# The output bias written into PSUM ahead of the output projection, with residuals, loads and banks moved around it

## The chip, the cores and the metric

The kernel runs on the eight cores of one Trainium2 chip. Every core computes one of the eight batch elements, and no core talks to another. The metric is the device time in microseconds of the slowest core. A line such as L517 names a line of the kernel before.

## The reference

For each batch element x is 4096 x 1024 in float32. One layer is computed, then a last RMSNorm:

```python
h = rmsnorm(x, norm_g)
proj = h @ w_in + b_in                       # 1024 -> 2816 columns
q, k, v, z_a, u, v_s, z_s = split(proj)      # 512,128,128,512,512,512,512
attn = banded_sink_attention(q, k, v, sinks) * silu(z_a)     # window 128, blocks of 128
sgu  = gelu(u) * (W_s @ layernorm(gelu(v_s)) + b) * silu(z_s) # chunks of 128
x = x + concat(attn, sgu) @ w_out + b_out
return rmsnorm(x, final_norm_g)
```

## The kernel before, in words

The 4096 rows of a core are eight stages of 512, and each stage is four tiles (or attention blocks) of 128 rows. A stage has these steps. The rows are loaded into `xa`, squared on ACT (L468), scaled to bf16 `xn` (L482, L483) and transposed into `xT`. TensorE then forms projections from `xT` in groups of eight matmuls, 512 columns each, one PSUM bank per group (`fm_group`, L517): four groups for q, one for k, four for u, four for z_s and four for z_a; v (L542) and v_s (L571) are formed row by row. ACT or DVE takes a group out of PSUM and adds its bias (L523, L524, L527). Attention of a block needs scores (L647), exp on ACT (L652), a mask (L665 on DVE or L660 on POOL), the sum of the two masked halves (L682), the products with v and with ones (L674, L677), ln and exp on ACT (L690, L694), and two multiplications (L696, L701) that end in `mixT`. The gating branch (L617 to L629) fills the other half of `mixT`.

The output of a row tile (`out_tile`) is two halves of 512 columns. For each half eight matmuls (L725) write one bank, and DVE adds the bank to the residual in `xe` (L730). ACT squares the tile (L733), POOL makes the reciprocal root in two small steps (L735, L737), DVE scales (L739) and SP stores it (L742). The residual is a second load of the same rows of x into `xe` (`load_xe`, L709), after which POOL adds the output bias to the whole tile in place (L711). `xe` has four tile slots, one for each tile of a stage; a slot is loaded again only when its store has been read out.

The order of instructions on every engine is fixed when the program is built. `Scheduler.run` is a list scheduler: it walks through time with a cost for each operation, takes the operation that can start first, and settles ties by a priority number. It also deals out the eight PSUM banks, by classes with caps: `CAPS = {"S": 4, "V": 2, "P": 4}`, where S is a pair of banks for scores, V the two banks of one attention block, and P all other groups, the output halves among them. ACT runs in phases per stage (gelu, silu, exp), with a table load between them (L424); the matmuls of a gelu or silu group are held back by `gate` until their phase is the current one or about to be. Each engine then runs its list in order, and waits for semaphores where an operand comes from elsewhere.

Setup: SP loads the 22 weight blocks of w_in through four slots of `xe` and four of `mixT`, POOL's own queue loads `w_out` with a cast to bf16 (L777, eight loads), and SP loads the small constants, among them `gf_sb` and `bout_sb` (L420).

## Time and profile before

| what | value |
|---|---|
| median of 3 runs | 534.2 us (534.0 to 534.81) |
| the profiled execution, its own time | 536.34 us |
| span of its slowest core (core 0), first to last instruction | 534.8 us |
| spans of all cores | 528.0 to 534.8 us |
| PE / DVE / ACT / POOL busy, share of the span | 90% / 71% / 61% / 36% |
| DMA, mean over the span | 137 GB/s |

The profile is of one execution. The span leaves out 1.5 us of that execution's own time. An engine that is busy for a small share of the whole can still set the end in one stretch, so the windows and the timeline are read beside the averages. Releasers in brackets say which instruction ended an idle time.

### The profile page before, as it was taken

The numbers are of one execution on the slowest core, as the hardware profiler recorded it, in microseconds if no ns is written. First come the engines' busy times: TensorE is split into PE (matmuls) and PEld (weight loads), VectorE is DVE, ScalarE is ACT, GpSimd is POOL, SyncE is SP. The second block draws the span as 40 slices with busy tenths as digits, with TensorE's granted clock in tenths as the row PEclk, the third lists the DMA queues.
The fourth block names the chain that finished last, engine by engine and source line by source line (L and its number), as shares of the span: only waits on it lengthen the run. The fifth ranks groups of instructions, "written<-read, shape, count | busy, mean of one in ns | idle before, by whom it ended". The sixth has DMA issues, their size and how long they took to land.

```text
span 534.8 us, 9042 instructions; the slowest of 8 cores (528.0 to 534.8 us)
## 1 busy us (share of the span) xinstructions
PE 483.6 (90%) x2802; PEld 221.5 (41%) x2852; DVE 379.2 (71%) x527; ACT 325.6 (61%) x565; POOL 191.6 (36%) x232
## 2 busy tenths in 40 slices
PE   1799986898999999999999999999999999999960
PEld 0357442344444434444444434443444435443320
DVE  1676889659778767778775597766757687557963
ACT  4363393855677475847675756858578575348621
POOL 1030564125023331333236254542364215450444
PEclk9999997999999999999999999999999999999985
DMA  7999993593008801336532933356342213300363
GB/s 233 329 344 324 313 232 50 106 253 116 1 40 203 230 1 40 120 66 172 159 104 59 210 101 119 119 94 146 126 152 65 51 63 136 119 1 39 120 182 132
DMA packets 44543, 73.12 MB, mean 137 GB/s; under 512 B 27600, under 2 KB 27728, under 8 KB 44496
## 3 DMA queue, kind: packets, MB, share of 16 engines
q1 hardware_dynamic: 43200, 70.40, 44.5%
q0 software_dynamic: 1152, 2.10, 2.4%
q8 instruction: 23, 0.38, 0.3%
q14 instruction: 24, 0.20, 0.1%
q10 hardware_dynamic: 144, 0.05, 0.1%
HBM read 51.56 MB, written 16.78 MB: 128 GB/s over the span
## 4 chain that ended last, share of the span: by engine, by line
PE 79%; issue 5%; DVE 4%; ACT 4%; POOL 3%; DMA 3%; SPq 0%; POOLq 0%; DVEq 0%; ACTq 0%
PE pp L517 40%; PE pp L725 18%; PE pp L571 9%; PE pp L674 3%; PE pp L647 3%; PE pp L542 2%; DMA xa<-x 2%; PE pp L556 1%; DMA xe<-x 1%; PE pp L677 1%; PE pp L617 1%; DVE PT L665 1%; DVE xe L739 1%; POOL w_out_bf L777 1%; ACT PT L652 1%
## 5 line engine op out<-in xcount | busy, mean ns | idle before, releaser
L517 PE MATMUL pp<-xT,w_fm 128*128 128x512 bf16 x1056 | 243.0, 382 | 6.9 <-DVE sgt L625 1.6
L517 PEld LDWEIGHTS pp<-xT,w_fm 128*128 128x128 bf16 x1088 | 104.2, 98 | 134.8 <-issue 15.9
L725 PE MATMUL pp<-w_out_bf,mixT 128*128 128x512 bf16 x497 | 117.8, 384 | 6.2 <-DVE mixT L701 3.8
L711 POOL TENSOR_TENSOR xe<-xe,bout_sb 128x1024 f32<-128x1024 f32 x32 | 77.4, 2423 | 29.7 <-DMA xe<-x 29.6
L725 PEld LDWEIGHTS pp<-w_out_bf,mixT 128*128 128x128 bf16 x512 | 47.9, 99 | 69.1 <-issue 18.0
L733 ACT ACTIVATE junk<-xe 128x1024 bf16<-128x1024 f32 x32 | 34.0, 1062 | 53.8 <-DVE xe L730 48.5
L730 DVE TENSOR_TENSOR xe<-pp,xe 128x512 f32<-128x512 f32 x64 | 43.4, 685 | 28.9 <-PE pp L725 24.1
L652 ACT ACTIVATE PT<-pp 128x1024 bf16<-128x1024 f32 x63 | 62.6, 1030 | 0.9 <-PE pp L647 0.9
L571 PE MATMUL pp<-w_vs,xT 128*128 128x512 bf16 x221 | 53.7, 391 | 6.6 <-DVE v_r L546 5.3
L739 DVE SCALAR_TENSOR_TENSOR xe<-xe,st_fr,gf_sb 128x1024 f32<-128x1024 f32 x32 | 47.1, 1473 | 15.4 <-POOL st_fr L737 9.5
L665 DVE TENSOR_TENSOR PT<-PT,pack_b_sb 128x1024 bf16<-128x1024 bf16 x57 | 50.4, 898 | 4.8 <-ACT PT L652 4.0
L690 ACT ACTIVATE LR<-pp,esink 128x128 f32<-128x128 f32 x128 | 36.3, 365 | 26.7 <-PE pp L677 26.0
L578 ACT ACTIVATE vs_f<-vs_f 128x512 f32<-128x512 f32 x32 | 19.6, 627 | 42.0 <-DVE vs_f L576 40.5
L735 POOL TENSOR_SCALAR st_fm<-st_fs 128x1 f32<-128x1 f32 x32 | 9.9, 309 | 95.9 <-ACT junk L733 95.4
L527 ACT ACTIVATE zaT<-pp,pack_a_sb 128x512 bf16<-128x512 f32 x32 | 21.7, 691 | 33.5 <-PE pp L517 32.2
L576 DVE TENSOR_TENSOR vs_f<-pp,bvs_sb 128x512 f32<-128x512 f32 x32 | 22.0, 688 | 26.1 <-PE pp L571 21.9
L468 ACT ACTIVATE junk<-xa 128x1024 bf16<-128x1024 f32 x32 | 33.7, 1055 | 6.0 <-DMA xa<-x 5.2
L571 PEld LDWEIGHTS pp<-w_vs,xT 128*128 128x128 bf16 x224 | 21.8, 100 | 35.5 <-issue 11.9
L629 POOL TENSOR_TENSOR mixT<-sgt,uT 128x512 bf16<-128x512 f32 x19 | 22.0, 1156 | 40.6 <-DVE sgt L625 33.8
L625 DVE SCALAR_TENSOR_TENSOR sgt<-pp,pack_b_sb,Cmat 128x512 f32<-128x512 f32 x32 | 23.2, 745 | 16.5 <-PE pp L617 8.9
L584 POOL TENSOR_SCALAR st_ve<-st_mv 128x1 f32<-128x1 f32 x32 | 8.5, 266 | 71.0 <-DVE st_mv L582 70.1
L424 ACT ACT_TABLE_LOAD x24 | 30.8, 1283 | 1.9 <-POOL ones L439 1.5
(63 smaller groups left out, 542.6 us busy)
## 6 DMA issues: line engine op xcount, KB each, us to landing
...
w_out_bf<-w_out POOLq DMA_DIRECT2D x8, 256.0 KB, 15.7
...
```

What stands on the lines that cost most here:

```text
L424: return lambda e: e.activation(out=dmy[:, 1:2], in_=dmy[:, 0:1], func=func)
L468: G.op("act", lambda e: e.activation(out=junk[:], in_=xa[:, tt, :], func=AF.Square, accum_out=st_ss[:, par, tt:tt + 1]), reads=[("xa", tt) ...
L517: ins = e.matmul(bank(h), lhsT=w_fm[:, FM.index(cb), k, :], rhs=xT[:, xb, k, :], start=(k == 0), stop=(k == 7))
L571: ins = e.matmul(bank(h), lhsT=xT[:, xb, k, tt * 128:(tt + 1) * 128], rhs=w_vs[:, k, :], start=(k == 0), stop=(k == 7))
L652: G.op("act", lambda e, h=h, kb=kb: e.activation(out=PT[:, p2, kb, :], in_=bank2(h), func=AF.Exp, scale=0.125), uses=[h], writes=[("PT", p ...
L665: return e.tensor_tensor(out=v, in0=v, in1=mask[kb].unsqueeze(1).to_broadcast([128, 8, 128]), op=ALU.mult)
L690: ins = e.activation(out=LR[:, lb, c * 128:(c + 1) * 128], in_=bank(hd)[:, c * 128:(c + 1) * 128], func=AF.Ln, bias=esink[:, c:c + 1])
L711: G.op("pool", lambda e: e.tensor_tensor(out=xe[:, s, :], in0=xe[:, s, :], in1=bout[:], op=ALU.add), reads=["c_bout"], writes=[("xe", s, 0 ...
L725: ins = e.matmul(bank(h), lhsT=mixT[:, mb, ec, tt * 128:(tt + 1) * 128], rhs=w_out[:, ec, hf * 512:(hf + 1) * 512], start=(ec == 0), stop= ...
L730: G.op("dve", lambda e, hf=hf, h=h: e.tensor_tensor(out=xe[:, s, hf * 512:(hf + 1) * 512], in0=bank(h), in1=xe[:, s, hf * 512:(hf + 1) * 5 ...
L733: G.op("act", lambda e: e.activation(out=junk[:], in_=xe[:, s, :], func=AF.Square, accum_out=st_fs[:, s:s + 1]), reads=[("xe", s, 0), ("xe ...
L739: G.op("dve", lambda e: e.scalar_tensor_tensor(out=xe[:, s, :], in0=xe[:, s, :], scalar=st_fr[:, s:s + 1], in1=gf[:], op0=ALU.mult, op1=AL ...
```

## The change

Six edits go together.

1. *Bias in PSUM.* POOL's addition of the bias (L711, 32 of them) goes. In its place ACT or DVE, whichever the scheduler finds free, copies 512 columns of the bias into the bank of an output half, 64 copies in all, and the eight matmuls of the half accumulate onto it (`start=False`). The copy reads the same inputs as the half needs, so it comes only when these are there. These banks are a class of their own, E, with a cap of 2, and they are only taken where the bank's last use wrote all of it by matmuls (`full`, `onto`). Where one bank is filled in pieces, only the first piece has `start` set.
2. *Last residual in `xa`.* The last stage has no load after it, so its rows are still in `xa`; its four tiles add onto `xa`, and are stored from there. Four loads of 512 KB go.
3. *Last silu inputs in SBUF.* The eight z groups of the last stage lose their gate. ACT or DVE takes them out of PSUM with their bias, into unused room of `xT` and of the q weights, and ACT applies silu from SBUF.
4. *`w_out` ahead of residual loads.* `gf_sb`, the first four loads of `xe` and the loads of `xa` for stage 2 all wait for the last load of `w_out`.
5. *Three V banks* instead of two.
6. *Port order.* A POOL operation marked `port` also waits for the DVE operation marked `port` that the scheduler placed ahead of it; L739 is now marked so.

```diff
-    CAPS = {"S": 4, "V": 2, "P": 4}
+    CAPS = {"S": 4, "V": 3, "P": 4, "E": 2}
...
+                    if b.onto and not all(bank_full[c] for c in cells):
+                        continue
...
             if o.port and e in ("dve", "pool"):
-                port[0] = free[e]
+                if e == "pool" and port[1] is not None and port[1].eng == "dve" and port[1] not in o.deps:
+                    o.deps.append(port[1])
+                port[:] = [free[e], o]
...
-            G.op("pe", mm, reads=[("xT", xb, t) for t in range(4)] + [("w", cb)], cost=1.73, alloc=[h], prio=prio, mode="full", gate=ph)
+            pre = st == NS - 1 and func == AF.Silu
+            G.op("pe", mm, reads=[("xT", xb, t) for t in range(4)] + [("w", cb)], cost=1.73, alloc=[h], prio=prio, mode="full",
+                 gate=None if pre else ph)
...
+                G.op({"dve": (0.745, lambda e: e.tensor_scalar(out=mem, in0=bank(h), scalar1=bias, scalar2=None, op0=ALU.add)),
+                      "act": (0.69, lambda e: e.activation(out=mem, in_=bank(h), func=AF.Identity, bias=bias))},
+                     None, uses=[h], reads=["c_biasfm"], writes=[("pre", i)], prio=prio, behind=[r for k in old for r in G.rd[k]])
+                G.op("act", lambda e: e.activation(out=dst, in_=mem, func=func), reads=[("pre", i)], writes=[key], cost=0.6,
+                     prio=prio - 0.3, phase=ph)
...
-            G.op("pool", lambda e: e.tensor_tensor(out=xe[:, s, :], in0=xe[:, s, :], in1=bout[:], op=ALU.add),
-                 reads=["c_bout"], writes=[("xe", s, 0), ("xe", s, 1)], cost=2.6, prio=st + 0.6 + 0.1 * s, port=True)
...
+            buf, key = (xa, ("xa", s)) if last else (xe, ("xe", s))
             for hf in range(2):
-                h = Bank("P")
...
+                h = Bank("E", onto=True)
...
+                fb = lambda e, h=h, cols=cols: e.activation(out=bank(h), in_=bout[:, cols], func=AF.Copy)
+                fv = lambda e, h=h, cols=cols: e.tensor_copy(out=bank(h), in_=bout[:, cols])
+                G.op({"act": (0.61, fb), "dve": (0.6, fv)}, None, reads=need + ["c_bout"], alloc=[h], prio=v0 - 0.2)
...
+                                       start=False, stop=(ec == 7), skip_group_check=True)
...
-            load_const("c_gf", gf[:], gf_d, eng="sp", kb=512, prio=-0.3, after=[w_op[21]])
+            load_const("c_gf", gf[:], gf_d, eng="sp", kb=512, prio=-0.3, after=[w_op[21]], reads=[("w_out", 7)])
...
         for cb in range(NCB):
             load_w(cb)
+        load_w_out()
...
         for tt in range(4):
-            load_xe(4 * (NS - 1) + tt)
             out_tile(4 * (NS - 1) + tt)
```

How the order moves, at three places. In the changed program L654, L694, L711, L658, L573, L725 and L604 are the old L625, L665, L682, L629, L546, L696 and L576; L757 is the new copy of the bias on DVE, L766, L730 and L775 are the old L730, L701 and L739, and L738, L440 and L431 the loads of L709, L429 and L420.

DVE, first attention stage, before (the masks of stage 0 and the v of stage 1):

```order
L625 SCALAR_TENSOR_TENSOR sgt<-pp,pack_b_sb,Cmat 128x512 [waits s_dve,s_pool,s_pe]
L523 TENSOR_SCALAR kT<-pp,pack_a_sb 128x512 [waits s_pe]
L665 TENSOR_TENSOR PT<-PT,pack_b_sb 128x1024 [waits s_act] x4
L682 TENSOR_TENSOR PC<-PT 128x1024 [waits s_dve]
L629 TENSOR_TENSOR mixT<-sgt,uT 128x512
L546 TENSOR_TENSOR v_r<-pp,pack_b_sb 128x512 [waits s_pe]
L625 SCALAR_TENSOR_TENSOR sgt<-pp,pack_b_sb,Cmat 128x512 [waits s_dve]
L576 TENSOR_TENSOR vs_f<-pp,bvs_sb 128x512 [waits s_pe]
```

DVE, the same place, with the change:

```order
L654 SCALAR_TENSOR_TENSOR sgt<-pp,pack_b_sb,Cmat 128x512 [waits s_dve,s_pool,s_pe]
L549 TENSOR_SCALAR kT<-pp,pack_a_sb 128x512 [waits s_pe]
L654 SCALAR_TENSOR_TENSOR sgt<-pp,pack_b_sb,Cmat 128x512 [waits s_dve,s_pool]
L694 TENSOR_TENSOR PT<-PT,pack_b_sb 128x1024 [waits s_act] x3
L711 TENSOR_TENSOR PC<-PT 128x1024 [waits s_dve]
L658 TENSOR_TENSOR mixT<-sgt,uT 128x512
L573 TENSOR_TENSOR v_r<-pp,pack_b_sb 128x512 [waits s_pe]
L694 TENSOR_TENSOR PT<-PT,pack_b_sb 128x1024 [waits s_act]
```

Three masks instead of four stand ahead of v_r, as one went to POOL, and the fourth sgt has moved ahead of them.

SP, the loads after the weights, before (`xa` is for stage 2, `xe` for the residual of stage 0; two more of `xe` follow):

```order
L420 DMA bout_sb<-bout_bc 128x1024
L420 DMA gf_sb<-gf_bc 128x1024
L429 DMA xa<-x 128x1024 [waits d_xa0,s_act]
L429 DMA xa<-x 128x1024 [waits d_xa1,s_act]
L429 DMA xa<-x 128x1024 [waits d_xa2,s_act]
L429 DMA xa<-x 128x1024 [waits d_xa3,s_act]
L709 DMA xe<-x 128x1024 [waits d_xe0,s_dve]
L709 DMA xe<-x 128x1024 [waits d_xe1,s_dve]
```

SP, the same place, with the change:

```order
L431 DMA bout_sb<-bout_bc 128x1024
L431 DMA gf_sb<-gf_bc 128x1024 [waits d_wo7]
L738 DMA xe<-x 128x1024 [waits d_xe0,s_dve]
L738 DMA xe<-x 128x1024 [waits d_xe1,s_dve]
L738 DMA xe<-x 128x1024 [waits d_xe2,s_dve]
L440 DMA xa<-x 128x1024 [waits d_xa0,s_act]
L738 DMA xe<-x 128x1024 [waits d_xe3,s_dve]
L440 DMA xa<-x 128x1024 [waits d_xa1,s_act]
L440 DMA xa<-x 128x1024 [waits d_xa2,s_act]
```

The load of gf waits for the last piece of `w_out` (d_wo7), and everything after it on SP stands behind that wait; the residual loads have moved ahead of those of `xa`.

DVE, last stage, before, around the attention blocks 2 and 3:

```order
L739 SCALAR_TENSOR_TENSOR xe<-xe,st_fr,gf_sb 128x1024 [waits s_pool,s_act]
L739 SCALAR_TENSOR_TENSOR xe<-xe,st_fr,gf_sb 128x1024 [waits s_pool,s_act,s_dve]
L701 TENSOR_TENSOR mixT<-pp,LR 128x4x128 [waits s_pool,s_pe]
L739 SCALAR_TENSOR_TENSOR xe<-xe,st_fr,gf_sb 128x1024 [waits s_pool,s_dve,s_act]
L696 TENSOR_TENSOR LR<-LR,zaT 128x512 [waits s_act]
L730 TENSOR_TENSOR xe<-pp,xe 128x512 [waits s_pool,s_pe]
L701 TENSOR_TENSOR mixT<-pp,LR 128x4x128 [waits s_dve,s_pe]
L730 TENSOR_TENSOR xe<-pp,xe 128x512
L739 SCALAR_TENSOR_TENSOR xe<-xe,st_fr,gf_sb 128x1024 [waits s_pool,s_dve,s_act]
L730 TENSOR_TENSOR xe<-pp,xe 128x512 [waits s_pool,s_pe]
```

DVE, last stage, with the change, around the same blocks:

```order
L766 TENSOR_TENSOR xe<-pp,xe 128x512 [waits s_pe]
L694 TENSOR_TENSOR PT<-PT,pack_b_sb 128x1024 [waits s_act]
L725 TENSOR_TENSOR LR<-LR,zaT 128x512 [waits s_act]
L766 TENSOR_TENSOR xe<-pp,xe 128x512 [waits s_pe,d_xe3]
L730 TENSOR_TENSOR mixT<-pp,LR 128x4x128 [waits s_dve,s_pe]
L757 COPY pp<-bout_sb 128x512 [waits s_pe]
L711 TENSOR_TENSOR PC<-PT 128x1024 [waits s_pool]
L725 TENSOR_TENSOR LR<-LR,zaT 128x512 [waits s_act]
L730 TENSOR_TENSOR mixT<-pp,LR 128x4x128 [waits s_dve,s_pe]
L766 TENSOR_TENSOR xa<-pp,xa 128x512 [waits s_pe,d_xa0]
L775 SCALAR_TENSOR_TENSOR xe<-xe,st_fr,gf_sb 128x1024 [waits s_pool,s_act]
L766 TENSOR_TENSOR xa<-pp,xa 128x512 [waits s_pe]
```

Copies of the bias now stand between the link from one block to the next, and the first two halves of the last stage are added to `xa`, ahead of the last block's L730.

## Rows read from the trace of the kernel before

**Rows 1.** The page, part 1: busy us, share of the span, instructions of each engine
```profile
PE 483.6 (90%) x2802; PEld 221.5 (41%) x2852; DVE 379.2 (71%) x527; ACT 325.6 (61%) x565; POOL 191.6 (36%) x232
```
**Rows 2.** Windows: each engine's busy time, granted clock, DMA share, GB/s, three stretches
```profile
60.00:90.00 30.00, 22.97 (x160) 10.74 (x162) 25.93 (x37) 19.02 (x32) 22.28 (x22) 0.92 0.84 195
150.00:490.00 340.00, 335.23 (x1874) 149.61 (x1908) 242.29 (x356) 224.32 (x392) 128.40 (x149) 1.00 0.37 106
490.00:534.80 44.80, 25.87 (x116) 10.14 (x116) 30.88 (x34) 17.64 (x38) 17.53 (x19) 0.82 0.41 141
```
**Rows 3.** Timeline 74 to 105: start us, us, instructions, count, [idle before <-releaser]
```profile
74.29 10.63 POOL L711 TENSOR_TENSOR xe<-xe,bout_sb 128x1024 f32<-128x1024 f32 x4
...
75.83 9.64 DVE L665 TENSOR_TENSOR PT<-PT,pack_b_sb 128x1024 bf16<-128x1024 bf16 x4
...
87.42 5.84 PE L571 MATMUL pp<-w_vs,xT 128*128 128x512 bf16 x16 [5.26 <-DVE v_r L546]
...
93.96 3.63 PE L725 MATMUL pp<-w_out_bf,mixT 128*128 128x512 bf16 x16
...
104.09 1.25 PE L517 MATMUL pp<-xT,w_fm 128*128 128x512 bf16 x5
```
**Rows 4.** Windows where the clock fell or transfers were dense, same columns
```profile
60.00:65.00 5.00, 4.95 (x30) 2.24 (x30) 3.52 (x8) 0.76 (x2) 4.74 (x7) 1.00 1.03 331
85.00:90.00 5.00, 2.58 (x7) 0.94 (x8) 5.00 (x9) 0.00 (x0) 1.81 (x2) 0.51 0.01 2
507.00:511.00 4.00, 1.02 (x8) 0.39 (x8) 3.56 (x3) 2.89 (x8) 3.38 (x4) 1.00 0.36 146
511.00:515.00 4.00, 3.97 (x12) 1.49 (x12) 3.99 (x3) 0.00 (x0) 2.09 (x1) 0.60 0.29 116
```
**Rows 5.** One line's instructions: ns min/median/max, first and last start
```profile
L665 DVE TENSOR_TENSOR PT<-PT,pack_b_sb x57: 678/684/2842, 75.8 to 500.0; 128x1024 bf16<-128x1024 bf16 x57
...
L739 DVE SCALAR_TENSOR_TENSOR xe<-xe,st_fr,gf_sb x32: 1269/1284/3165, 104.7 to 530.4; 128x1024 f32<-128x1024 f32 x32
```
**Rows 6.** Groups by line and shape: busy us, mean ns, idle before
```profile
L711 POOL TENSOR_TENSOR xe<-xe,bout_sb 128x1024 f32<-128x1024 f32 x32 | 77.4, 2423 | 29.7 <-DMA xe<-x 29.6
...
L578 ACT ACTIVATE vs_f<-vs_f 128x512 f32<-128x512 f32 x32 | 19.6, 627 | 42.0 <-DVE vs_f L576 40.5 <-DVE st_mv L582 1.5
```
**Rows 7.** Timeline of the last stage, columns as in rows 3
```profile
476.75 5.13 PE L517 MATMUL pp<-xT,w_fm 128*128 128x512 bf16 x23 [0.16 <-issue]
...
484.08 3.77 ACT L652 ACTIVATE PT<-pp 128x1024 bf16<-128x1024 f32 x4
...
489.48 0.39 PE L647 MATMUL pp<-qT,kT 64*128 64x512 bf16 x2
...
500.04 2.84 DVE L665 TENSOR_TENSOR PT<-PT,pack_b_sb 128x1024 bf16<-128x1024 bf16 x1
...
507.18 0.63 PE L674 MATMUL pp<-PT,v_r 128*64 128x512 bf16 x4
...
507.63 0.39 PE L677 MATMUL pp<-PC,ones 128*64 128x512 bf16 x2
...
511.03 8.81 PE L725 MATMUL pp<-w_out_bf,mixT 128*128 128x512 bf16 x31 [3.01 <-DVE mixT L701]
...
526.37 1.29 DVE L730 TENSOR_TENSOR xe<-pp,xe 128x512 f32<-128x512 f32 x2 [1.02 <-POOL xe L711]
```
**Rows 8.** Chain that ended last, near its end: start us, us, what
```profile
514.70 6.73 DMA xe<-x
...
521.56 2.35 POOL xe L711
```
**Rows 9.** The page, part 3: the software queue, packets, MB, share of 16 engines
```profile
q0 software_dynamic: 1152, 2.10, 2.4%
```
**Rows 10.** The tile w_out_bf, first 120 us: its loads, and issue to landing
```profile
L777 POOL DMA_DIRECT2D w_out_bf<-w_out x8: 535/557/760, 60.1 to 67.5; - x8
...
DMA to landing us min/median/max: 9.0/15.7/18.2
```

More of the change, by code:

```diff
@@ L70, in op @@
     def op(self, eng, fn, reads=(), writes=(), cost=0.1, prio=0.0, alloc=(), uses=(), phase=None, gate=None, mode=None,
-           dsem=None, kb=0, final=False, after=(), port=False):
+           dsem=None, kb=0, final=False, after=(), port=False, behind=()):
         o = Op()
@@ L86, in op @@
             deps[id(w)] = w
+        for r in behind:
+            deps[id(r)] = r
         o.deps = list(deps.values())
@@ L138, in run @@
         mode = [None]
-        port = [0.0]
+        port = [0.0, None]
         def when(o, e):
@@ L236, in run @@
                         bank_owner[c] = b
+                        bank_full[c] = b.full
                         for u in bank_last[c]:
@@ L495, in transpose_x @@
                 return
-            h = Bank("P")
+            h = Bank("P", full=False)
             def tr(e):
@@ L719, in out_tile, with mmo @@
                 v0 = st + 0.3 + 0.1 * tt
+            last = st == NS - 1
+            buf, key = (xa, ("xa", s)) if last else (xe, ("xe", s))
             for hf in range(2):
-                h = Bank("P")
-                def mmo(e, hf=hf, h=h):
+                h = Bank("E", onto=True)
+                cols = slice(hf * 512, (hf + 1) * 512)
+                need = [("mixA", mb, tt)] + [("mixS", mb, jj) for jj in range(4)] + [("w_out", k) for k in range(8)]
+                fb = lambda e, h=h, cols=cols: e.activation(out=bank(h), in_=bout[:, cols], func=AF.Copy)
+                fv = lambda e, h=h, cols=cols: e.tensor_copy(out=bank(h), in_=bout[:, cols])
+                G.op({"act": (0.61, fb), "dve": (0.6, fv)}, None, reads=need + ["c_bout"], alloc=[h], prio=v0 - 0.2)
+                def mmo(e, cols=cols, h=h):
@@ L724, in mmo @@
                     for ec in range(8):
-                        ins = e.matmul(bank(h), lhsT=mixT[:, mb, ec, tt * 128:(tt + 1) * 128], rhs=w_out[:, ec, hf * 512:(hf + 1) * 512],
-                                       start=(ec == 0), stop=(ec == 7))
-                    return ins
-                G.op("pe", mmo, reads=[("mixA", mb, tt)] + [("mixS", mb, jj) for jj in range(4)] + [("w_out", k) for k in range(8)],
-                     cost=1.73, alloc=[h], prio=v0 + 0.05 * hf, mode="full")
-                G.op("dve", lambda e, hf=hf, h=h: e.tensor_tensor(out=xe[:, s, hf * 512:(hf + 1) * 512], in0=bank(h),
-                                                                  in1=xe[:, s, hf * 512:(hf + 1) * 512], op=ALU.add),
-                     uses=[h], writes=[("xe", s, hf)], cost=0.68, prio=v0 - 0.5)
@@ L733, in out_tile @@
-            G.op("act", lambda e: e.activation(out=junk[:], in_=xe[:, s, :], func=AF.Square, accum_out=st_fs[:, s:s + 1]),
-                 reads=[("xe", s, 0), ("xe", s, 1)], writes=["junk", ("fs", s)], cost=1.25, prio=v0)
+                        ins = e.matmul(bank(h), lhsT=mixT[:, mb, ec, tt * 128:(tt + 1) * 128], rhs=w_out[:, ec, cols],
+                                       start=False, stop=(ec == 7), skip_group_check=True)
+                    return ins
+                G.op("pe", mmo, reads=need, writes=[("oT", h)], cost=1.73, uses=[h], prio=v0 + 0.05 * hf, mode="full")
@@ L788, in build_program @@
         setup_late()
-        load_w_out()
         gelu_part(0)
```

49 lines of the change are left out of this document (33 added, 16 removed).

## The prediction

> **What bounds the kernel now.** I read the page first: PE is busy 90% of the span, the next engine 71% [rows 1]. The windows show that this average hides three different kernels [rows 2]. From 150 to 490 us PE is busy 335.23 of 340 us at a granted clock of 1.00: it idles 4.8 us in five and a half stages, and no other engine's saving can buy more than that there. From 60 to 90 us it idles 7.0 us, and in the last 44.8 us it idles 18.9. So a gain has to come from two places, the first attention stage and the tail, or from nowhere.
>
> *The first attention stage.* The timeline [rows 3] shows DVE with four masks (L665) in 9.64 us, from 75.83. One such mask takes 0.68 us when nothing is beside it, and up to 2.84 [rows 5]. What is beside these four is POOL's bias addition (L711), four of them in 10.63 us from 74.29. v_r stands behind the masks in DVE's list, and PE waits 5.26 us for it (L571). The wait also costs clock: the granted clock is 0.51 from 85 to 90 [rows 4], and the 16 matmuls from 87.42 take 5.84 us.
>
> *The tail.* The last projection matmul ends at 476.75 + 5.13 = 481.88 [rows 7], and the span lasts 52.9 us more. The chain near the end [rows 8] is a load of `xe` issued at 514.70 and landing 6.73 us later, then POOL's 2.35 us of bias: the slot was free only after the store of the stage before. PE is done with its last matmul at 519.84 (511.03 + 8.81) [rows 7], so these 15 us to the end are mostly residual, not work.
>
> **The change, part by part.**
>
> *Bias through PSUM.* Removed: 32 POOL instructions of 2.42 us, 77.4 us [rows 6]. Added: 64 copies of 128x512, in the new order 41 on ACT and 23 on DVE. No row shows a copy from SBUF into PSUM. The nearest is ACT's gelu from SBUF to SBUF on the same shape, 0.63 us [rows 6]; the other bound is the addition out of PSUM at 0.60 us from one to the next (the pair at 526.37: 1.29 for two of 0.69 [rows 7]). I take 0.61; ends this near change nothing. That is 26 us on ACT, which is busy 66% of the middle stretch, and 14 on DVE, 71% [rows 2], which gets back what POOL's long additions took from it: its masks mean 0.90 against 0.68 alone, a 57-fold 0.2 us. PE waits for a copy where it wasn't scheduled long enough ahead. In PE's new list 31 of the 64 output halves carry no wait at all (before: 17), as an earlier matmul had already waited for something later; of the 33 that do, 4 stand in the first attention stage and 14 in the tail. In the middle I therefore take 0, between a gain of 2 us (half of the 4.8) and a loss of 4 (48 halves at under 0.1).
>
> *First attention stage.* I follow the new lists with the measured durations, from 75.8 us. The fourth sgt (0.75), three masks (0.68 each), PC, mixT and v_r (0.6 from one to the next) end v_r near 80.5. The v_s matmuls wait for that bank or the one before it and start at 80.6. Two blocks' products and three v_s groups bring PE to 87, the link of ln, exp and two multiplications of the first block is done, and the first copy of the bias ends near 89.5. The first output half starts at 89.6, the last block's products at 93.2, and the 24 projection matmuls at 96.0, with three output halves done. Before, they start at 104.09 [rows 3] with four done, of 1.7 us each (5.13 / 24 x 8) [rows 7]. The gain is 104.1 - 1.7 - 96.0 = **6.4 us**. Its upper end is all that PE loses there: 7.0 us idle [rows 2] and 5.84 - 3.4 = 2.4 to the clock, 9.4. Its lower end is 0, below.
>
> *Loads.* In the new list SP stops at gf until the last piece of `w_out` has landed. POOL issues these pieces from 60.1 to 67.5, as before [rows 10]. Their packets took 2.4% of 16 engines' 534.8 us, 12.8 us of everything [rows 9], now with nearly nothing beside them, so I put the landing at 75. Then nine loads of 512 KB at 331 GB/s [rows 4], 1.6 us each: the third tile of `xa` at about 90, the last at 92. ACT's list wants them at 91 to 95. Cost 0, with 2 to 3 us in hand; the cover is PE's own work, and without it what is late is ACT's ln of the last block, which stands behind three squares of `xa`.
>
> *Last silu inputs in SBUF, third V bank.* The eight groups can run before their phase, but PE had nothing to fill there (the middle stretch). What moves is one output half more into the tail (16 after the last projection matmul, before 15), so that matmul comes 1.7 us earlier. In exchange the last group goes through SBUF: from PE's end to the first exp there were 484.08 - 481.88 = 2.2 us [rows 7], and one silu from SBUF, 0.63, with its hand-over makes it 3.0.
>
> *The tail, counted from the end of the last projection matmul.* PE works through seven halves, eight score pairs and three blocks' products without a long wait, to about 20.4 us. Then it waits for the copy that stands on DVE behind the link of block 1 (the order excerpt), to 23.1. One half, and block 3's products end at 25.9; before, they end at 508.02 - 481.88 = 26.1 [rows 7]: here next to nothing is won, since the mask at 500.04 that took 2.84 us is shorter by 2.2 but the halves stand ahead of the blocks. From there the kernels part. Before, 26.8 us follow. Now eight halves follow on two banks: copy 0.6, matmuls 1.7 and 0.2 more until they land, addition 0.7, hand-overs, 3.6 us a bank, 1.8 a half; L739 (1.28 alone [rows 5]) pushes in front of two additions and costs 0.3 to 0.6. The last matmul ends at 40.5. From the start of the last addition to the end took 534.8 - 526.97 = 7.8 us [rows 7], so the end is at 48.4. That is 52.9 - 48.4 = **4.5 us**. The upper end is a PE that never waits: 16 halves (27.4), eight score pairs of 0.39, four blocks' products of 0.84 [rows 7] and 7.8 of ending, 41.7, a gain of 11.2. The lower end is DVE late for every one of the last eight: 2.5 us a half, 48.4 + 5.6 = 54, a loss of 1.1.
>
> *Sum.* 6.4 + 1.7 + 4.5 = 12.6 us. The profiled execution took 536.34 us for its span of 534.8; taken from its own time that is 523.7. The median is 2.1 under it, and I forecast 534.2 - 12.6 = **521.6 us**. Bounds added: 9.4 + 1.7 + 11.2 + 2 off gives 509.9; 0 + 1.7 - 1.1 - 4 gives 537.6.
>
> **The rivals.**
>
> *PE never waits in the tail.* For it: the residual and POOL are gone from the chain, and 14 of 16 halves lie behind one another in PE's list. Against: two banks. With most of the 6.7 us between 4.5 and 11.2 it gives 515.6.
>
> *`w_out` lands late.* If it lands at 84, as it could have before (67.5 plus up to 18 us [rows 10]), the ACT squares run to 101 and the gain of the first stage is gone: 528. Against: DMA was at 1.03 share then [rows 4], with residual loads that now come later. The Trainium skill (SBUF — State Buffer, Who interferes with whom) has a reason why it could come so: a load issued from GpSimd's queue starves of descriptors while DVE holds the port they share. Its transfers from 60 to 65 us ran at full share here [rows 4], so no row shows it.
>
> *The clock falls in front of output halves, slower than before.* A bank must now be copied before PE may use it. If that makes PE idle, the clock can fall: after 5.26 us of idle before 87.42 the granted clock is 0.51, the lower of its two levels (1.2 of 2.4 GHz), and after 3.01 before 511.03 it is 0.60, mostly that level [rows 3, 4, 7]. One such fall costs the idle, 3.0 us, and 5.84 - 3.4 = 2.4 on the next 16 matmuls, 5.4 us. Two undo 10.8 of the 12.6; from the third on the change is slower, 537.8, and one in each of seven stages would give 559. Against: 31 halves without a wait, and a middle stretch at 1.00. The Trainium skill (TensorE: Matmul & The Clock Gate, A second HAM failure mode) describes this for cycling through PSUM banks with small idle times between groups. By that rule the change is on the wrong side; the middle of this trace cycles its banks at a full clock.
>
> **How the numbers follow.** My forecast, 517 to 526: 0.60. PE never waiting, 512 to 517: 0.13. `w_out` late or DVE late in the tail, 526 to 531: 0.15. The clock or waits in the middle, over 535.3: 0.08. No change: 0.04, where the gains and a part of the losses meet. A measurement of this kernel tells about 0.2%, 1.1 us, from no change. Faster 0.88, same 0.04, slower 0.08. The range 514 to 529 leaves out the last two and the ends of the middle cases.
>
> **What would show it.** Right: masks at 0.68 us in the first attention stage, no wait of PE for v_r, projection matmuls of stage 1 going on near 96; no load and no POOL work in the chain of the last 30 us; in the tail PE's waits fall on DVE's or ACT's copies, a few tenths each. Wrong: PE idle above 10 us between 150 and 470; ACT waiting for `xa` at 95; the clock below 1.00 in the middle; additions of the last stage more than 1 us behind their matmuls.

## The result and the profile after

The changed kernel takes 529.46 us (median; 528.57 to 530.89) where the kernel before takes 534.5 (534.0 to 534.81) on the same chip: a ratio of 0.9909, 95% interval 0.9885 to 0.9933, 0.9% faster. On a second chip it was 528.27 against 535.42, ratio 0.9866 (0.9841 to 0.989). Executions in which one half of the chip showed a lower granted clock and took longer are left out of all medians and ratios here. The forecast was 521.6, in a range of 514 to 529: right in sign, too far by 7 to 8 us. The profiled execution took 528.57 us with a span of 526.8, on core 3. From here on a line number without a note is one of the changed kernel.

The page's first part, after (against [rows 1]):

```profile
span 526.8 us, 9311 instructions; the slowest of 8 cores (520.1 to 526.8 us)
PE 490.3 (93%) x2852; PEld 221.7 (42%) x2852; DVE 358.0 (68%) x553; ACT 353.5 (67%) x611; POOL 103.1 (20%) x200
```

POOL has lost its additions, ACT has gained 24 us of copies (41 of 0.60 us) and DVE 16 (23 of 0.69 us), and PE is at 93%. To see where time went, I cut each core's span in three at two places of PE's timeline: **S** is the start of the 32 stage-1 projection matmuls behind the first attention stage (L528; L517 before), **M** the time from there to the end of the last projection matmul, and **T** the rest, the tail. The table gives the median of the eight cores of a profiled execution, and their range. At S three output halves are done after and four before, and in T 16 are left after and 15 before, so that M holds the same work.

| kernel | S | M | T | spans of the cores |
|---|---|---|---|---|
| before (forecast's profile) | 103.7 (100.8 to 105.2) | 376.4 | 51.4 (50.4 to 52.9) | 528.0 to 534.8 |
| after | 97.5 (95.0 to 100.5) | 376.2 | 49.3 (48.3 to 49.6) | 520.1 to 526.8 |

The typical core gained 8.8 us (531.8 to 523.0). But the time is that of the slowest core, and over the executions of this first comparison the slowest stood 4.5 us above the median core (523.3), where it stood 2.5 above in the kernel before (b1, below): the cores now differ in S.

PE of the slowest core, timeline between the attention stage and stage 1:

```profile
85.39 0.39 PE L676 MATMUL pp<-qT,kT 64*128 64x512 bf16 x2
89.11 6.23 PE L762 MATMUL pp<-w_out_bf,mixT 128*128 128x512 bf16 x16 [3.33 <-DVE PT L694]
95.28 0.62 PE L703 MATMUL pp<-PT,v_r 128*64 128x512 bf16 x4
...
96.05 1.90 PE L762 MATMUL pp<-w_out_bf,mixT 128*128 128x512 bf16 x8
100.45 8.75 PE L528 MATMUL pp<-xT,w_fm 128*128 128x512 bf16 x32 [2.50 <-ACT LR L719]
```

DVE in the same stretch:

```profile
76.23 1.94 DVE L694 TENSOR_TENSOR PT<-PT,pack_b_sb 128x1024 bf16<-128x1024 bf16 x3
...
79.30 0.68 DVE L573 TENSOR_TENSOR v_r<-pp,pack_b_sb 128x512 bf16<-128x512 f32 x1
...
87.44 0.69 DVE L757 COPY pp<-bout_sb 128x512 f32<-128x512 f32 x1
88.03 0.68 DVE L694 TENSOR_TENSOR PT<-PT,pack_b_sb 128x1024 bf16<-128x1024 bf16 x1
```

The long wait for v_r [rows 3] is gone, and two others have come: 3.33 us in front of the first output half, and 2.50 us for ACT's ln of block 3 (L719). The first is put down to a mask (L694), which stands right behind the copy of the bias (L757) in DVE's list; that the copies hold PE there is shown by e4 and e6 below, where the wait falls to 1.17 and 0.45 us. Behind the first wait, 16 matmuls take 6.23 us instead of 3.6, behind the second 32 take 8.75 instead of 7.07. ACT in the same stretch shows what ln stands behind:

```profile
87.99 0.63 ACT L756 ACTIVATE pp<-bout_sb 128x512 f32<-128x512 f32 x1
94.33 1.06 ACT L479 ACTIVATE junk<-xa 128x1024 bf16<-128x1024 f32 x1 [5.71 <-DMA xa<-x]
...
96.89 1.06 ACT L479 ACTIVATE junk<-xa 128x1024 bf16<-128x1024 f32 x1 [1.41 <-DMA xa<-x]
...
98.13 1.06 ACT L479 ACTIVATE junk<-xa 128x1024 bf16<-128x1024 f32 x1
...
99.18 1.12 ACT L719 ACTIVATE LR<-pp,esink 128x128 f32<-128x128 f32 x4
```

The squares of `xa` for stage 2 wait for loads, and ln, whose input PE had at 96, stands behind three of them. SP's issues tell why the loads are late (start, time of the issue):

```profile
46.27 0.73 SPq L431 DMA_DIRECT2D bout_sb<-bout_bc  x1
78.47 0.33 SPq L431 DMA_DIRECT2D gf_sb<-gf_bc  x1
78.96 2.57 SPq L738 DMA_DIRECT2D xe<-x  x3
81.67 0.34 SPq L440 DMA_DIRECT2D xa<-x  x1
82.16 0.34 SPq L738 DMA_DIRECT2D xe<-x  x1
82.65 1.70 SPq L440 DMA_DIRECT2D xa<-x  x3
```

From 47 to 78.5 us SP does nothing: gf waits for the last piece of `w_out` (edit 4), and eight loads stand behind it. The chain of waits (start, length, what) passes through one of them, the second tile of `xa`, issued at 82.65:

```profile
82.65 14.10 DMA xa<-x
```

The windows (length, PE's busy time with the number of its matmuls, granted clock, DMA share, GB/s):

```profile
85.00:90.00 5.00, 1.67 (x11) 0.76 1.08 268
90.00:95.00 5.00, 5.00 (x15) 0.56 0.91 344
...
150.00:450.00 300.00, 299.39 (x1695) 1.00 0.39 117
478.30:526.80 48.50, 35.96 (x169) 0.91 0.22 87
```

The middle is as it was, and at full clock. In the tail no load and no POOL addition is in the way any more; PE has one long wait for a copy:

```profile
499.72 2.71 PE L762 MATMUL pp<-w_out_bf,mixT 128*128 128x512 bf16 x8 [2.36 <-DVE pp L757]
...
503.79 5.46 PE L762 MATMUL pp<-w_out_bf,mixT 128*128 128x512 bf16 x24
509.53 7.07 PE L762 MATMUL pp<-w_out_bf,mixT 128*128 128x512 bf16 x32 [0.28 <-DVE pp L757]
516.75 1.89 PE L762 MATMUL pp<-w_out_bf,mixT 128*128 128x512 bf16 x8 [0.15 <-DVE pp L757]
```

### The profile page after: what moved, and what is told of

It reads as the page before. It is cut to its first block, busy times and chain, and to the rows that moved or that the text cites. A ratio compares the mean times of both kernels' runs of the same rounds, so it can differ in the third digit from the quotient of the medians.

```text
span 526.8 us, 9311 instructions; the slowest of 8 cores (520.1 to 526.8 us)
## 1 busy us (share of the span) xinstructions
PE 490.3 (93%) x2852; PEld 221.7 (42%) x2852; DVE 358.0 (68%) x553; ACT 353.5 (67%) x611; POOL 103.1 (20%) x200
## 4 chain that ended last, share of the span: by engine, by line
PE 85%; DMA 4%; DVE 3%; ACT 3%; issue 2%; POOL 1%; SPq 1%; POOLq 0%; DVEq 0%; ACTq 0%
PE pp L528 45%; PE pp L762 20%; PE pp L599 8%; DMA xa<-x 4%; PE pp L676 3%; PE pp L703 3%; PE pp L568 2%; PE pp L583 1%; PE pp L706 1%; PE pp L645 1%; ACT junk L479 1%; DVE xa L775 1%; DVE sgt L654 1%; ACT xn L493 0%; SPq L738 0%
## 5 line engine op out<-in xcount | busy, mean ns | idle before, releaser
L528 PE MATMUL pp<-xT,w_fm 128*128 128x512 bf16 x1088 | 248.8, 383 | 5.5 <-ACT LR L719 2.5
L528 PEld LDWEIGHTS pp<-xT,w_fm 128*128 128x128 bf16 x1088 | 104.2, 99 | 137.1 <-issue 19.3
L762 PE MATMUL pp<-w_out_bf,mixT 128*128 128x512 bf16 x512 | 123.1, 388 | 6.1 <-DVE PT L694 3.3
L766 DVE TENSOR_TENSOR xe<-pp,xe 128x512 f32<-128x512 f32 x56 | 38.5, 688 | 27.8 <-PE pp L762 26.2
L606 ACT ACTIVATE vs_f<-vs_f 128x512 f32<-128x512 f32 x32 | 19.9, 627 | 45.6 <-DVE vs_f L604 41.6
L719 ACT ACTIVATE LR<-pp,esink 128x128 f32<-128x128 f32 x128 | 36.5, 369 | 16.7 <-PE pp L706 16.1
L775 DVE SCALAR_TENSOR_TENSOR xe<-xe,st_fr,gf_sb 128x1024 f32<-128x1024 f32 x28 | 35.9, 1281 | 16.8 <-POOL st_fr L773 15.2
L771 POOL TENSOR_SCALAR st_fm<-st_fs 128x1 f32<-128x1 f32 x32 | 6.1, 190 | 192.6 <-ACT junk L769 81.8
L479 ACT ACTIVATE junk<-xa 128x1024 bf16<-128x1024 f32 x32 | 33.6, 1050 | 12.7 <-DMA xa<-x 12.6
L694 DVE TENSOR_TENSOR PT<-PT,pack_b_sb 128x1024 bf16<-128x1024 bf16 x58 | 39.0, 686 | 3.3 <-ACT PT L681 2.8
L604 DVE TENSOR_TENSOR vs_f<-pp,bvs_sb 128x512 f32<-128x512 f32 x32 | 22.0, 688 | 26.2 <-PE pp L599 23.6
L769 ACT ACTIVATE junk<-xe 128x1024 bf16<-128x1024 f32 x28 | 29.6, 1059 | 9.8 <-DVE xe L766 8.8
L654 DVE SCALAR_TENSOR_TENSOR sgt<-pp,pack_b_sb,Cmat 128x512 f32<-128x512 f32 x32 | 23.3, 748 | 15.5 <-POOL mixT L658 9.5
L658 POOL TENSOR_TENSOR mixT<-sgt,uT 128x512 bf16<-128x512 f32 x22 | 25.5, 1157 | 30.2 <-DVE sgt L654 19.4
L756 ACT ACTIVATE pp<-bout_sb 128x512 f32<-128x512 f32 x41 | 24.2, 599 | 6.3 <-DVE xe L766 5.1
L608 DVE BATCH_NORM_STATS2 st_bn<-vs_f 128x6 f32<-128x512 f32 x32 | 21.6, 684 | 9.3 <-ACT vs_f L606 9.3
## 6 DMA issues: line engine op xcount, KB each, us to landing
xe<-w_in SPq DMA_DIRECT2D x12, 512.0 KB, 12.8
LR<-sgu_wT SPq DMA_DIRECT2D x1, 512.0 KB, 12.8
```

The source lines that it names most:

```text
L479: G.op("act", lambda e: e.activation(out=junk[:], in_=xa[:, tt, :], func=AF.Square, accum_out=st_ss[:, par, tt:tt + 1]), reads=[("xa", tt) ...
L528: ins = e.matmul(bank(h), lhsT=w_fm[:, FM.index(cb), k, :], rhs=xT[:, xb, k, :], start=(k == 0), stop=(k == 7))
L654: G.op("dve", lambda e, jj=jj, h=h, sb_=sb_: e.scalar_tensor_tensor(out=sgt[:, sb_, :].rearrange("p (c t) -> p c t", c=4), in0=bank(h).rea ...
L694: return e.tensor_tensor(out=v, in0=v, in1=mask[kb].unsqueeze(1).to_broadcast([128, 8, 128]), op=ALU.mult)
L719: ins = e.activation(out=LR[:, lb, c * 128:(c + 1) * 128], in_=bank(hd)[:, c * 128:(c + 1) * 128], func=AF.Ln, bias=esink[:, c:c + 1])
L762: ins = e.matmul(bank(h), lhsT=mixT[:, mb, ec, tt * 128:(tt + 1) * 128], rhs=w_out[:, ec, cols], start=False, stop=(ec == 7), skip_group_c ...
```

## The experiments

A new planner's run would move instructions everywhere, so the experiments let the scheduler run as it is and then edit its finished lists. `keep` holds the operations by name: `"xa", st, tt` loads, `"cp", n, hf` copies, `"half", n, hf` matmuls of a half, `"ex", n` the exp behind ln, `"mk", n` the later mask, `"pv", n` the products. All dependences stay with an operation when it moves. Theory A: late loads, through ACT's list. Theory B: the copies, PE's idle time in front of the first half and the clock behind it. Ratios are to the kernel before, with 95% intervals; 0.001 is 0.54 us.

| run | edit | ratio (interval) | median us | S (range) | M | T |
|---|---|---|---|---|---|---|
| b1 | kernel before again | 0.9997 (0.9983 to 1.0011) | 535.72 | 104.6 (102.5 to 105.6) | 377.7 | 51.0 |
| b2 | changed kernel again | 0.9866 (0.9841 to 0.989) | 528.27 | 97.9 (93.9 to 98.9) | 376.2 | 48.6 |
| e1 | xa loads early | 0.9841 (0.9815 to 0.9867) | 527.71 | 97.5 (95.5 to 98.9) | 377.6 | 48.6 |
| g3 | e1 again | 0.9825 (0.9807 to 0.9842) | 526.06 | 96.9 (94.8 to 99.0) | 376.2 | 48.7 |
| e2 | ln first | 0.9917 (0.9888 to 0.9945) | 531.5 | 96.7 (94.2 to 99.5) | 380.6 | 48.6 |
| e3 | no wait for w_out | 0.9866 (0.9839 to 0.9893) | 528.71 | 98.8 (96.7 to 100.1) | 376.2 | 49.3 |
| e4 | copies early | 0.9882 (0.9863 to 0.9902) | 529.08 | 96.8 (91.9 to 100.3) | 377.7 | 48.6 |
| g2 | e1 + e4 | 0.9774 (0.9752 to 0.9796) | 522.83 | 94.0 (92.9 to 95.6) | 376.2 | 48.9 |
| e5 | g2 + third half early | 0.9765 (0.9744 to 0.9786) | 522.54 | 94.5 (92.7 to 95.1) | 376.1 | 49.4 |
| h3 | e5 again | 0.9774 (0.976 to 0.9789) | 523.34 | 94.9 (94.0 to 96.6) | 376.1 | 48.8 |
| e6 | no copies | 0.9816 (0.9794 to 0.9838) | 525.9 | 97.8 (93.0 to 100.7) | 377.9 | 45.3 |
| h1 | e5, no copies | 0.9685 (0.9671 to 0.97) | 518.09 | 94.0 (93.1 to 94.9) | 376.2 | 45.5 |
| g1 | before, no bias on POOL | 0.9745 (0.9729 to 0.976) | 521.63 | 96.7 (95.3 to 98.6) | 375.0 | 46.1 |
| g4 | e5, last bias on POOL | 0.9739 (0.9723 to 0.9754) | 521.45 | 94.1 (93.9 to 96.0) | 378.6 | 45.6 |
| h2 | g4, other places | 0.9702 (0.9687 to 0.9716) | 519.42 | 94.4 (92.8 to 95.4) | 376.2 | 45.5 |

**b1 and b2, the two kernels again.** No edit.

> The kernel before, once more, so that the spans of its eight cores stand beside those of the changed kernel, whose typical core (median over its four runs) takes 523.3 us and whose slowest takes 4.5 us more. Theory A (the start of stage 1 is scattered by late loads in the changed kernel, and the slowest core sets the time): the typical core of the kernel before takes 530.5 to 532 and its slowest 1.5 to 3 us more, so that the typical core gained about 8 us and the slowest only 5. Theory B (the terms themselves are too large): the typical core takes 528 to 529.5, the gain is about 5 us on every core, and the spread is the same in both kernels.

> The changed kernel once more, on the chip of the three runs beside it, with the spans of its cores. From the first comparison: 529.5 us against 534.5, typical core (median over runs and cores) 523.3, the slowest of a run 4.5 above it. Theory A (late xa scatters the start of stage 1): again 4 us or more between the typical core and the slowest, ratio to before 0.989 to 0.992. If this chip gives the same 0.984 as e1_xa_early had, e1 gained nothing.

The kernel before: median core 531.75, slowest 2.5 above. The changed kernel: median core 523.3 as in the first comparison, slowest 3.2 above, and a ratio under the range that I expected. So 8.4 us on the typical core is firm, and the slowest core got 5 to 7 of them.

**e1, early loads of `xa`.**

```diff
+for o in xa2: no_wout(o); order["sp"].remove(o)   # xa2 = keep["xa", 2, 0..3]
+at = order["sp"].index(keep["c_gf"])
+order["sp"][at:at] = xa2
```

> The changed kernel with SP's list alone altered: the four loads of xa for stage 2 stand ahead of gf and don't wait for w_out. Theory A (these loads come late, and ACT's ln of block 3 stands behind the squares that wait for them): xa is there by 88, PE no longer waits for L719, the stage-1 matmuls L528 start at 95 to 96.5 on all cores instead of 95.0 to 100.5, and the time falls from 529.5 to 525.5 to 527.5. Theory B (PE's idle time of 3.3 us and the low clock ahead of the first output half cost it, the loads are hidden): xa is early and the time stays within 0.5 us of 529.5. Theory C (the loads take w_out's room): w_out lands 3 us later or more, the first output half starts after 91, and the time is 529.5 to 532.

> e1 once more, beside g2 on the same chip: 0.982 to 0.986 of the kernel before, with the start of L528 at 95.5 to 99, PE idle for 3.34 us in front of the first half on every core and the 16 matmuls behind it at 3.6 us on some cores and 4.9 to 6.4 on others.

The wait for ln is gone on every core of both profiles, so A holds for that wait. But the start missed its 95 to 96.5, and the ratios, 0.0025 and 0.004 under b2's, aren't clear of it: both intervals overlap b2's, g3's by 0.0001. S stays scattered, since the other cost stands alone now. Core 5 of e1:

```profile
90.10 6.32 PE L762 MATMUL pp<-w_out_bf,mixT 128*128 128x512 bf16 x16 [3.34 <-DVE PT L694]
...
98.87 7.07 PE L528 MATMUL pp<-xT,w_fm 128*128 128x512 bf16 x32
```

M is 1.4 us longer in e1 than in b2: near 300 us five of eight cores have one more wait of PE, 1.4 to 3.3 us, on four of them for a transposing DMA into `xT`. Core 5, the slowest, is so for this reason too. Core 1 of b2 has the same wait without the edit (1.62 us); why it comes stays open.

**e2, ln ahead of the squares.**

```diff
+sq = [...]   # the four squares of xa, stage 2
+for o in sq: order["act"].remove(o)
+at = order["act"].index(keep["ex", 3]) + 1
+order["act"][at:at] = sq
```

> The changed kernel with ACT's list alone altered: ln and exp of block 3 of stage 0 stand ahead of the four squares of xa instead of behind three of them; all loads are as late as in the changed kernel. Theory A: PE's wait for L719 goes as in e1, the start of L528 moves to 95 to 97 by core and the time falls by 1.5 to 3 us, to 526.5 to 528; what is left to e1 is the gelu of stage 1, which now stands behind the squares. Theory B: within 0.5 us of 529.5. If e1 gains and this doesn't, the late xa hurts somewhere else than through ACT's ln.

A miss. The start moves to 94.2 to 99.5, but M grows by 4.4: the gelu of stage 1 now waits behind the late squares, and PE for gelu. Core 4:

```profile
95.49 5.34 PE L528 MATMUL pp<-xT,w_fm 128*128 128x512 bf16 x24
104.41 3.16 PE L528 MATMUL pp<-xT,w_fm 128*128 128x512 bf16 x8 [3.57 <-ACT uT L553]
```

So the late load itself is what costs, wherever ACT meets it.

**e3, no load waits for `w_out`.**

```diff
+for o in [keep["c_gf"]] + xa2 + [keep["xe", n] for n in range(4)]: no_wout(o)
```

> The changed kernel with the same lists on every engine, but gf, xe and xa don't wait for the last piece of w_out, so SP issues them from about 62 on beside it. Theory A: xa lands before 88 and the gain is that of e1 (525.5 to 527.5) unless w_out is what becomes late. Theory C (the wait protects w_out: twelve loads beside it): w_out lands 8 us later or more, at 84 to 90, the first output half starts at 91 or later, and the time is 530 to 533.

Between A and C: 0.9866. `w_out` lands after 16.3 to 17.9 us by core (median of its pieces from issue) instead of 6.3 to 9.6 in the changed kernel, the first half starts at 90.5 (median of the cores) instead of 89.2 in b2, the wait for ln is gone, and against b2 nothing is gained or lost that can be told. So edit 4 protects `w_out` and holds `xa`, and here the two cancel.

**e4, the first two copies early.**

```diff
+move(keep["cp", 0, 0], behind=...)   # its last dependence on DVE, a v_s addition
+move(keep["cp", 0, 1], behind=keep["ex", 1])
```

> The changed kernel with the copies of the bias for the first two output halves moved ahead in DVE's and ACT's lists, to where their inputs are ready (on DVE behind the second v_s addition, on ACT behind the exp of block 1); loads as in the changed kernel. In its trace these copies run some 3 us after the inputs are there, PE idles 3.34 us in front of the first half on every core, and on seven of eight cores the next 16 matmuls take 4.9 to 6.4 us instead of 3.6. Theory B (this idle time and the clock behind it are the loss): the first half starts 2.5 to 3.3 us earlier, PE's idle time is under 1 us, and the start of L528 and the time fall by 2 to 3.5 us, where no load holds them; the ratio falls by 0.004 to 0.006. Theory A alone (late xa, ACT's ln behind squares): the first half starts earlier, PE waits longer for L719, and the time falls by less than 1 us.

A's reading: 0.9882, no gain. The first half starts 2.8 us earlier than in b2, with 1.17 us of idle time, and its 16 matmuls take 3.6 us on all cores. Then PE waits longer for ln, 1.9 to 6.0 us on seven of eight cores, and on five of them the 32 matmuls behind that wait take 8.5 to 9.9 us instead of 7.07. Core 3:

```profile
87.28 3.61 PE L762 MATMUL pp<-w_out_bf,mixT 128*128 128x512 bf16 x16 [1.17 <-DVE vs_f L604]
...
92.42 1.89 PE L762 MATMUL pp<-w_out_bf,mixT 128*128 128x512 bf16 x8 [0.76 <-DVE pp L757]
100.35 9.32 PE L528 MATMUL pp<-xT,w_fm 128*128 128x512 bf16 x32 [6.04 <-ACT LR L719]
```

**g2 and e5, both together.** e5 also moves the third half:

```diff
+move(keep["cp", 1, 0], behind=keep["mk", 3])
+move(keep["half", 1, 0], before=keep["pv", 3])
```

> e1 and e4 together (loads of xa for stage 2 ahead of gf and not behind w_out; first copies early), and the third output half with its copy moved ahead of the last block's products, since its inputs are ready too. If both causes hold (A and B), they add: no wait for L719, no idle time of 3.3 us, 16 matmuls in 3.6, L528 starts at 92.5 to 94.5 on most cores instead of 95.0 to 100.5, and the time is 5 to 7 us under the changed kernel's, ratio 0.977 to 0.981. If only A holds: the ratio of e1, 0.984. If the time freed at the start is given back later (a wait for xT or for copies in stage 1): the start moves and the distance from the start to the end of the last projection matmul grows from 376.2.

> The changed kernel with e1's early loads of xa and e4's early copies, without the third half moved as in e5. e1 alone had a ratio of 0.984, e4 alone 0.988, the changed kernel 0.987 to 0.991, e5 0.9765. If late loads and late copies hide each other (each alone shows the other), most of e5's gain is here: L528 starts at 94.0 to 96.5, no 16 matmuls at the low clock on most cores, ratio 0.978 to 0.981. If the third half is what gains: ratio of 0.982 or more.

> e5 once more, on the chip of the two beside it: ratio 0.975 to 0.979, cores within 3 us of each other, start of L528 at 92.5 to 95.5 on every core.

Both causes hold: 0.9774 and 0.9765, where the single edits gave 0.983 and 0.988, with intervals that don't meet. From e4 to g2 the early loads are worth 0.0108, 5.8 us, and from e1 and g3 to g2 the early copies 0.0051 to 0.0067, 2.7 to 3.6 us. Each hid the other. The third half adds nothing that can be told. In e5 S is within 3 us on all cores, and so are the spans (517.9 to 520.7). Core 3 of e5:

```profile
87.64 5.34 PE L762 MATMUL pp<-w_out_bf,mixT 128*128 128x512 bf16 x24 [1.17 <-DVE vs_f L604]
92.91 0.63 PE L703 MATMUL pp<-PT,v_r 128*64 128x512 bf16 x4
...
95.13 7.07 PE L528 MATMUL pp<-xT,w_fm 128*128 128x512 bf16 x32 [1.38 <-ACT LR L719]
```

**e6 and h1, no copies**, in the changed kernel and in e5.

```diff
-start=False, stop=(ec == 7)
+start=(ec == 0), stop=(ec == 7)
+order[e] = [o for o in order[e] if id(o) not in gone]   # gone: the 64 copies
```

> The changed kernel without the 64 copies: the first matmul of a half starts its bank anew, the lists are otherwise the same. Left out: the output bias. This prices the copies. My forecast had them at nothing in the middle and about 4 us in the tail (bank time 3.6 us for two banks, 3.0 without a copy; waits of 2.7 and 0.7 us). Theory B says that they also cost the 3.3 us in front of the first half. So the tail shrinks from 49 by 3 to 5 us, the first half starts 2 to 3 us earlier, the middle stays at 376.2, and the time is 4 to 8 us under the changed kernel's. If copies are hidden everywhere: within 1 us.

> e5 without the 64 copies. Left out: the output bias. This splits what the changed kernel gives back against the kernel before without its additions on POOL (g1, 0.9745) into the copies and the loads. e5 minus this is what copies cost where no load is late; e6 (0.9816, no copies but late loads) minus this is what late loads cost. If the copies cost mainly in the tail (49.3 to 45.2 us in e6) and at the first halves: start of L528 at 92 to 94, 376 to the last projection matmul, 45.2 behind it, time 517 to 519, ratio 0.966 to 0.970. If copies are cheap once the loads are early: 521.5 to 523, ratio 0.974 to 0.977.

Both leave out the output bias. The tail is 45.3 to 45.5, as expected: copies cost it 3.3 to 4 us. But e6 takes only 2.7 us less than b2 (0.005), not the 4 to 8 that I expected: the early first half is lost again to the late loads, and M grows by 1.7, as the clock falls behind that wait on six of eight cores. Core 7 waits 7.43 us:

```profile
100.64 9.70 PE L528 MATMUL pp<-xT,w_fm 128*128 128x512 bf16 x32 [7.43 <-ACT LR L719]
```

With early loads the copies cost 0.9774 - 0.9685 = 0.0089, 4.8 us (h3 against h1, same chip), most of it in T. Without copies the late loads cost 0.9816 - 0.9685 = 0.0131, 7.0 us. Their sum, 11.8, is the size of the 10 to 12 us between h1 and the changed kernel.

**g1, the kernel before without POOL's additions.**

```diff
+gone = {id(o): o for o in keep.values()}   # the 32 additions of L711
+order["pool"] = [o for o in order["pool"] if id(o) not in gone]
```

> The kernel before without POOL's 32 bias additions (L711); all other lists are the same. Left out: the output bias. It prices what the removal of POOL's work is worth alone, with no copies put in its place and none of the other five edits. My forecast laid the whole first term on it: masks at 0.68 us, no wait of PE for v_r, and the stage-1 projections L517 start 5 to 7 us earlier, at 97 to 99 instead of 103 to 105; in the tail the loads of xe stay in the chain and only 2.35 us of POOL go, so the tail falls from 51.4 to 48.5 to 50. Time 7 to 9 us under the kernel before, ratio 0.983 to 0.987. Rival (POOL only seems to hold DVE, the loads of xe and w_out hold the stage): start earlier by less than 3 us, ratio over 0.991.

More than expected: 0.9745, 13.7 us. S falls by 7 to 8, M by 1.4 or more, T by 5, where I had expected 1 to 3 of T; why it is more isn't shown. Core 0, DVE and then PE (line numbers of the kernel before; against [rows 3]):

```profile
76.61 2.49 DVE L665 TENSOR_TENSOR PT<-PT,pack_b_sb 128x1024 bf16<-128x1024 bf16 x4
...
80.22 0.68 DVE L546 TENSOR_TENSOR v_r<-pp,pack_b_sb 128x512 bf16<-128x512 f32 x1
```

```profile
82.88 3.63 PE L571 MATMUL pp<-w_vs,xT 128*128 128x512 bf16 x16
...
98.14 7.08 PE L517 MATMUL pp<-xT,w_fm 128*128 128x512 bf16 x31
```

The four masks take 2.49 us instead of 9.64. Removing POOL's work, with none of the other edits, is worth all that I forecast for the change; the rest of the change, which puts the bias back, gives 6 to 9 us of it away again.

**g4 and h2, the last stage's bias on POOL.** A version to beat both: e5, without the eight copies of the last stage. POOL adds the bias to `xa` ahead of time, four additions.

```diff
+o.fn = lambda e, s=s: e.tensor_tensor(out=xa[:, s, :], in0=xa[:, s, :], in1=bout[:], op=ALU.add)
+at = order["pool"].index(keep["fr", 20 + s]) + 1                       # g4
+at = ... keep["fr", 20]) - 1 if s < 2 else ... keep["fr", 23]) + 1     # h2
```

> e5, and in the last stage the bias doesn't come by copies: POOL adds it to the four tiles of xa in the middle of stage 6, once they are scaled, 2.4 us each, where POOL has nothing else for 5 us or more, and the first matmul of a half starts its bank anew. If the copies bound the tail (e6 without any: 45.2 us behind the last projection matmul instead of 49.3), the tail falls to 45.5 to 47 us and the time to 518.5 to 520.5, ratio 0.970 to 0.973. If POOL's additions hold DVE's masks of stage 6 so long that PE waits for them, the distance from the start of L528 to the end of the last projection grows above 376.2 by 1 to 4 us and eats it.

> g4 with POOL's four additions at other places: two right behind the last product of the gating branch of stage 6, two behind the last output tile of stage 5, where DVE has less work on bf16 masks. In g4 each stood beside masks and the scaling of an output tile (L775 took 2.67 us instead of 1.28, masks 0.94 instead of 0.69) and the distance from the start of L528 to the last projection matmul grew by 2 to 3 us. If these neighbours are the cause: that distance is 376.2 to 377.5 and the time 519 to 520.5, ratio 0.969 to 0.972. If any 2.4 us of POOL beside DVE costs the same wherever it stands: 0.974 as g4.

In both the tail is 45.5. In g4 the middle pays 2.4 us for it. DVE's groups from 400 to 470 us on core 2, of e5 and then of g4 (busy, mean ns | idle before):

```profile
L775 DVE SCALAR_TENSOR_TENSOR xe<-xe,st_fr,gf_sb 128x1024 f32<-128x1024 f32 x4 | 5.1, 1280 | 2.6 <-POOL st_fr L773 2.6
L766 DVE TENSOR_TENSOR xe<-pp,xe 128x512 f32<-128x512 f32 x7 | 4.8, 690 | 4.4 <-PE pp L762 4.4
L694 DVE TENSOR_TENSOR PT<-PT,pack_b_sb 128x1024 bf16<-128x1024 bf16 x7 | 4.8, 685 | 0.3 <-ACT PT L681 0.2
```

```profile
L775 DVE SCALAR_TENSOR_TENSOR xe<-xe,st_fr,gf_sb 128x1024 f32<-128x1024 f32 x4 | 10.7, 2673 | 1.8 <-POOL st_fr L773 1.8
L694 DVE TENSOR_TENSOR PT<-PT,pack_b_sb 128x1024 bf16<-128x1024 bf16 x7 | 6.6, 937 | 0.3 <-ACT PT L681 0.2
L766 DVE TENSOR_TENSOR xe<-pp,xe 128x512 f32<-128x512 f32 x7 | 4.8, 683 | 2.0 <-PE pp L762 2.0
```

L775 and the masks, which read two tiles of SBUF, grow to 2.67 and 0.94 us; the addition out of PSUM, which reads one, stays at 0.68. The Trainium skill (SBUF — State Buffer, Who interferes with whom) says this of the two: an instruction of VectorE with two inputs in SBUF contends with one of GpSimd that reads SBUF; one with a single such input, outside the 2-port modes, doesn't. These rows agree. In h2 the same four additions stand where DVE has less of that kind, and M is back at 376.2. h2 takes 519.42 us, ratio 0.9702 (0.9687 to 0.9716), 3.0% faster than the kernel before, faster than the changed kernel too, and 1.3 us above h1, which has no bias at all. Eight halves run without a gap there, on core 7:

```profile
494.64 13.99 PE L762 MATMUL pp<-w_out_bf,mixT 128*128 128x512 bf16 x64
```

Not tried: edits 2, 3, 5 and 6 one by one. h1 is 3.2 us faster than g1, and which of them, or of the moved loads, that comes from stays open.

## Why the prediction was right and wrong

*Masks and v_r: right.* In the changed kernel masks take 0.68 us, v_r is done at 79.98 on core 3 (80.5 by forecast), and g1 shows that POOL's additions were the cause of the wait.

*"Cost 0, with 2 to 3 us in hand" for the loads: wrong, and the main failure.* I had `w_out` landing at 75 and the third tile of `xa` at about 90. SP went on at 78.47, the second tile landed at 96.75 (82.65 + 14.10), and the third square started at 98.13: 3.5 us of this are the late start, the rest is the rate, as the DMA moved 250 GB/s from 78.47 to 96.75 where I had 331. I had named the cover (PE's own work) and what is late without it (ln of block 3 behind three squares), and that is what came. The late loads cost 5.8 us where copies are early (e4 to g2) and 7.0 without copies (e6 to h1). Rival 2 had the squares "run to 101" and 528 us. Both numbers came (101.3 on core 3), but the time with some luck: `w_out` landed at 78, not 84, and the gain of the first stage, which that rival had gone, stayed at 4.5 us by medians, while the tail gave 2 us less than forecast. I gave that case 0.15 together with DVE late in the tail; a cover of 2 us against an unknown landing deserved more.

*Three output halves at 1.7 us each: wrong by the clock.* Of the two ways to lose, I took only PE's idle time (2.6 us in front of the first half by my times, 3.3 measured). On seven of eight cores the 16 matmuls behind it took 4.9 to 6.4 us instead of 3.6, and on core 3 the granted clock was 0.56 from 90 to 95. I had this mechanism as the rival that ends slower, and put none of it into the sum; it came at one or two places of the first stage on seven of eight cores and once in the tail, not in each stage. With the loads early, moving the copies got back 2.7 to 3.6 us of idle time and clock (e1 and g3 to g2). The Trainium skill (TensorE: Matmul & The Clock Gate, A second HAM failure mode) describes a clock that goes up and down in a kernel that cycles through PSUM banks, from small idle times between groups. Nothing of the kind came in the middle of this kernel: with its copies it stayed at 1.00, PE was busy 299.39 of 300 us, so it hardly idled between groups, and in the changed kernel's two profiles the clock fell only behind single idle times of 2.36 us and more.

*Middle 0: right* (376.4 to 376.2).

*Tail 48.4: right as a time, mis-sized as a gain.* It is 48.5 on core 3 and 48.3 to 49.6 on all. But I subtracted it from 52.9, core 0's tail, where the seven others have 50.4 to 51.5. What made core 0's longer isn't shown: its link had a mask of 2.84 us, but three of the others had one of 2.62 to 2.72. The term of 4.5 is 2.1 by medians. The wait for the copy behind the link of block 1, 2.7 us by forecast, is 2.36. What copies cost in T, 3.3 to 4 us, is mostly this wait and the low clock behind it (eight matmuls in 2.71 us instead of 1.9): from the last score pair to the last eight halves it is 8.2 us on core 3, and 5.5 in e6 on core 7, which has shorter waits in that place. On the last eight halves it is 0.85 us (503.79 to 518.64, against 14.0 in h2).

*The sum.* Forecast 6.4 + 1.7 + 4.5 = 12.6. Measured by medians of cores: 103.7 - 1.7 - 97.5 = 4.5, then 1.7, 0.2 and 2.1, 8.5. Of the rest of the miss, 0.7 to 2 us are the spread: 3.2 to 4.5 us from the median core to the slowest, 2.5 before. The landing of the late loads and the fall of the clock differ by core, and the slowest sets the time; in e5, without either in the first stage, the spread is 1.4. About 1 us isn't accounted for. With both losses of the first stage gone (g2) the time is 522.83, 1.2 us from the forecast, but by other terms: the first stage gives 8.0 (103.7 - 1.7 - 94.0) and the tail 2.5, where I had 6.4 and 4.5.
